# Every third low part of the weights in the second FFN loop, made by an accumulating transfer instead of VectorE

## What is computed

```python
h2 = _rms(x, g_norm2) * (1 + sc2) + sh2
gate, up = jnp.split(h2 @ w_ffn_in, 2, axis=-1)     # w_ffn_in: 2048 x 11264
x = x + gt2 * ((jax.nn.silu(gate) * up) @ w_ffn_out)  # w_ffn_out: 5632 x 2048
```

## Time and profile before

| | us |
|---|---|
| median of 2 runs | 2519.33 (2518.88 to 2519.78) |
| span of the profiled execution | 2517.7 |
| PE busy | 2440.5 (97%) |
| DVE busy | 1793.1 (71%) |
| ACT busy | 1082.6 (43%) |
| POOL busy | 223.2 (9%) |

### The profile page before, as it was taken

One profiled execution on the slowest core, in us unless ns is written; L12 is line 12 of the kernel. 1 busy time (PEld: TensorE's weight loads), 2 busy tenths in 40 slices (PEclk: granted clock), 3 DMA queues, 4 the chain that ended last, 5 costly groups with the idle time before them and its releaser, 6 DMA issues.

```text
span 2517.7 us, 30560 instructions
## 1 busy us (share of the span) xinstructions
PE 2440.5 (97%) x11620; PEld 2000.9 (79%) x11620; DVE 1793.1 (71%) x1751; ACT 1082.6 (43%) x1243; POOL 223.2 (9%) x397
## 2 busy tenths in 40 slices
PE   4899999999999999999999999999999999999999
PEld 3679448888888888879997778788788888888887
DVE  6878887888888888778785445865688555555565
ACT  2035124444444444464346557644544444444443
POOL 4412210111111111001110000000011000000000
PEclk8899999999999999999999999999999999999999
DMA  9999996898889888647985555355588555555654
GB/s 367 382 337 354 403 358 225 308 328 313 312 321 328 317 318 323 209 152 279 341 291 162 166 172 161 117 184 200 198 320 285 191 192 185 197 184 192 208 184 150
DMA packets 291262, 643.01 MB, mean 255 GB/s; under 512 B 21883, under 2 KB 34749, under 8 KB 290269
## 3 DMA queue, kind: packets, MB, share of 16 engines
q1 hardware_dynamic: 234512, 436.45, 50.8%
q0 software_dynamic: 56096, 205.02, 21.8%
q10 hardware_dynamic: 556, 0.18, 0.0%
HBM read 639.47 MB, written 2.13 MB: 255 GB/s over the span
## 4 chain that ended last, share of the span: by engine, by line
PE 86%; DVE 5%; DMA 4%; ACT 4%; issue 1%; POOL 0%; DVEq 0%; ACTq 0%; POOLq 0%
PE PS L1783 84%; DMA R<-in_w_ada 3%; DVE R L1093 2%; ACT WHI L580 1%; DVE WLO L1073 1%; DMA RAW<-in_w_ffn_gate 1%; PE PS L2013 1%; PE PS L1907 1%; PE PS L1938 0%; DVE H L1243 0%; ACT R L658 0%; ACT L945 0%; ACT L588 0%; DVE H L1242 0%; ACT L937 0%
## 5 line engine op out<-in xcount | busy, mean ns | idle before, releaser
L1073 DVE TENSOR_TENSOR WLO<-RAW,WHI 128x1024 fp32r<-128x1024 f32 x760 | 929.7, 1225 | 610.3 <-ACT WHI L580 608.0
L580 ACT ACTIVATE WHI<-RAW 128x1024 fp32r<-128x1024 f32 x760 | 805.5, 1061 | 1118.3 <-PE PS L1783 1103.0
L1783 PE MATMUL PS<-WHI,H 128*128 128x512 f32 x4064 | 1263.1, 392 | 5.7 <-DVE WLO L1073 5.0
L1783 PEld LDWEIGHTS PS<-WHI,H 128*128 128x128 f32 x4064 | 755.0, 188 | 173.8 <-DVE WLO L1073 16.0
L1783 PE MATMUL PS<-WLO,H 128*128 128x512 f32 x2032 | 792.1, 390 | 0.0
L1783 PEld LDWEIGHTS PS<-WLO,H 128*128 128x128 f32 x2032 | 381.4, 188 | 80.8
L1093 DVE SCALAR_TENSOR_TENSOR R<-R,CA 128x1024 f32<-128x1024 f32 x326 | 417.6, 1281 | 36.7 <-DMA R<-in_w_ada 29.7
L1783 PE MATMUL PS<-WHI,HID 128*128 128x512 f32 x1280 | 395.2, 390 | 0.0
L514 POOL DMA_DIRECT2D R<-in_w_ada x284 | 150.9, 531 | 1586.7 <-DVE R L1090 555.1
L1783 PEld LDWEIGHTS PS<-WHI,HID 128*128 128x128 f32 x1280 | 239.3, 188 | 49.0
L1783 PE MATMUL PS<-WLO,HID 128*128 128x512 f32 x640 | 249.1, 389 | 0.0
(11 more groups left out here) (233 smaller groups left out, 1233.7 us busy)
## 6 DMA issues: line engine op xcount, KB each, us to landing
R<-in_w_ada POOLq DMA_DIRECT2D x348, 512.0 KB, 6.7
RAW<-in_w_in SPq DMA_DIRECT2D x88, 1024.0 KB, 5.6
RAW<-in_w_ffn_in SPq DMA_DIRECT2D x88, 1024.0 KB, 5.0
RAW<-in_w_ffn_gate SPq DMA_DIRECT2D x44, 1024.0 KB, 6.9
RAW<-in_w_ffn_up SPq DMA_DIRECT2D x44, 1024.0 KB, 5.3
RAW<-in_w_ffn_down SPq DMA_DIRECT2D x44, 1024.0 KB, 8.3
RAW<-in_w_ffn_out SPq DMA_DIRECT2D x44, 1024.0 KB, 5.0
RAW<-in_w_out SPq DMA_DIRECT2D x32, 1024.0 KB, 7.3
```

The lines of the kernel that those rows point to most:

```text
L580: nc.scalar.activation(WHI[j][:, :, :], RAW[slot][:, 2 * half:2 * half + 2, :], ACT.Copy)\
L1073: nc.vector.tensor_tensor(WLO[j][:, :, :], RAW[slot][:, 2 * half:2 * half + 2, :], WHI[j][:, :, :].bitcast(F32), ALU.subtract).then_inc(lo ...
L1783: return nc.tensor.matmul(o, a, b, start=start, stop=stop, skip_group_check=True)
```

## The change

In turns 3 to 8 of the second layer's FFN, for the subs whose number counted from 616 leaves 2 when divided by 3 (48 of 144, 8 in a turn), DVE makes no low part. ACT writes WHI[j] as before and then, with a second pass over the same source, -RAW rounded to fp32r into WLO[j]. POOL waits for that (`neg_done`) and issues a transfer from RAW (SBUF) to WLO[j] (SBUF) that adds: WLO = -WHI + RAW. It counts `lo_pool` by 16 when it has landed, and PE waits for that semaphore ahead of such a sub. SP waits for both kinds of low part before it reloads a slot. PE counts the two kinds apart (`lows`, `pool_lows`). SP's loop is written out for layer two, since its waits differ from turn to turn, and ACT's loop starts at 3 instead of 2, with turn 2 written out, in both layers.

```diff
--- before.py
+++ after.py
@@ -116,6 +116,19 @@
+POOL_LO = (2 * U_FFN2 + 64, 2 * U_FFN2 + 64 + 24 * (NF - 5))
+def on_pool(s):
+    return POOL_LO[0] <= s < POOL_LO[1] and (s - POOL_LO[0]) % 3 == 2
+def pool_before(s):
+    return (max(0, min(s, POOL_LO[1]) - POOL_LO[0])) // 3
 def ring(s):
@@ -161,8 +174,10 @@
         self.quad, self.chain = Count(), Count()
+        self.lows, self.pool_lows = Count(), Count()
         self.all = dict(unit=self.unit, sub=self.sub, A=self.A, B=self.B, C=self.C, ada=self.ada,
-                        ada_group=self.ada_group, gate=self.gate, hid=self.hid, quad=self.quad, chain=self.chain)
+                        ada_group=self.ada_group, gate=self.gate, hid=self.hid, quad=self.quad, chain=self.chain,
+                        lows=self.lows, pool_lows=self.pool_lows)
@@ -290,6 +305,7 @@
         hi_done, lo_done, pe_sub = sem("hi_done"), sem("lo_done"), sem("pe_sub")
+        lo_pool, neg_done = sem("lo_pool"), sem("neg_done")
         pe_tb = sem("pe_tb")
@@ -353,7 +369,10 @@
                 elif last >= 0:
-                    sp.wait_ge(lo_done, c.unit.value(-3, times=2) - native_before(last))
+                    pooled_lows = pool_before(last + 2)
+                    sp.wait_ge(lo_done, c.unit.value(-3, times=2) - native_before(last) - pooled_lows)
+                    if pooled_lows:
+                        sp.wait_ge(lo_pool, 16 * pooled_lows)
                 c.unit.at += 1
@@ -389,11 +408,16 @@
                 down(0)
-                with sp.Fori(2, NF - 2) as i:
-                    c.enter(i - 2, unit=12)
-                    gate_up(i)
-                    down(i - 1)
-                c.leave(NF - 4)
+                if k == 3:
+                    for i in range(2, NF - 2):
+                        gate_up(i)
+                        down(i - 1)
+                else:
+                    with sp.Fori(2, NF - 2) as i:
+                        c.enter(i - 2, unit=12)
+                        gate_up(i)
+                        down(i - 1)
+                    c.leave(NF - 4)
                 gate_up(NF - 2)
@@ -558,6 +582,21 @@
+            def lows(n):
+                for s in range(n):
+                    if on_pool(c.sub.at):
+                        half, slot = c.sub.at % 2, c.sub.at // 2 % 4
+                        j, _ = ring(c.sub.at)
+                        pool.wait_ge(neg_done, c.pool_lows.value(1))
+                        pool.dma_start(WLO[j][:, :, :].bitcast(F32), RAW[slot][:, 2 * half:2 * half + 2, :], accum_op=ALU.add)\
+                            .then_inc(lo_pool, 16)
+                        c.pool_lows.at += 1
+                    c.sub.at += 1
+            c.sub.at = 2 * U_FFN2 + 64
+            lows(24 * (NF - 5))
@@ -579,6 +618,9 @@
                         .then_inc(hi_done, 1)
+                    if on_pool(c.sub.at):
+                        nc.scalar.activation(WLO[j][:, :, :], RAW[slot][:, 2 * half:2 * half + 2, :], ACT.Copy, scale=-1.0)\
+                            .then_inc(neg_done, 1)
                     c.sub.at += 1
@@ -742,10 +784,11 @@
                 body()
-                with act.Fori(2, NF - 2) as i:
-                    c.enter(i - 2, unit=12, sub=24, hid=1, gate=1)
+                body()
+                with act.Fori(3, NF - 2) as i:
+                    c.enter(i - 3, unit=12, sub=24, hid=1, gate=1)
                     body()
-                c.leave(NF - 4)
+                c.leave(NF - 5)
                 body(rows=True)
@@ -1069,9 +1112,10 @@
                     j, _ = ring(c.sub.at)
-                    dve.wait_ge(hi_done, c.sub.value(1) - native_before(c.sub.at))
-                    nc.vector.tensor_tensor(WLO[j][:, :, :], RAW[slot][:, 2 * half:2 * half + 2, :],
-                                            WHI[j][:, :, :].bitcast(F32), ALU.subtract).then_inc(lo_done, 1)
+                    if not on_pool(c.sub.at):
+                        dve.wait_ge(hi_done, c.sub.value(1) - native_before(c.sub.at))
+                        nc.vector.tensor_tensor(WLO[j][:, :, :], RAW[slot][:, 2 * half:2 * half + 2, :],
+                                                WHI[j][:, :, :].bitcast(F32), ALU.subtract).then_inc(lo_done, 1)
                     c.sub.at += 1
@@ -1782,10 +1826,20 @@
+            def low_ready(more=0):
+                at = c.sub.at + more
+                if on_pool(at):
+                    pe.wait_ge(lo_pool, c.pool_lows.value(1, times=16))
+                    c.pool_lows.at += 1
+                else:
+                    pe.wait_ge(lo_done, c.lows.value(1))
+                    c.lows.at += 1
             def sub(pair, src, k0, first, last, kind="W", counted=True):
                 (j, _), used, o = ring(c.sub.at), c.all[pair], PAIR[pair]
-                pe.wait_ge(lo_done, c.sub.value(1) - native_before(c.sub.at))
+                low_ready()
                 if first and used.at:
@@ -1825,7 +1879,7 @@
                                 middle()
-                            pe.wait_ge(lo_done, c.sub.value(i + 1) - native_before(c.sub.at))
+                            low_ready(i)
                         if i == 1:
@@ -2041,7 +2095,9 @@
                 with pe.Fori(3, NF - 2) as i:
-                    c.enter(i - 3, sub=24, A=2, C=2, hid=1, gate=1, ada_group=1 * beside)
+                    pooled_lows = 8 if k == 3 else 0
+                    c.enter(i - 3, sub=24, A=2, C=2, hid=1, gate=1, ada_group=1 * beside, lows=24 - pooled_lows,
+                            pool_lows=pooled_lows)
                     gate(previous)
```

## The result

| | before | after |
|---|---|---|
| median, us | 2519.33 (2518.88 to 2519.78) | 2628.01 (2627.02 to 2628.99) |
| span of the profiled execution, us | 2517.7 | 2627.3 |
| ratio, 95% interval | | 1.0431 (1.0414 to 1.0449) |

The account below looks back on a forecast made before the run. PE was taken to bound the loop, so relieving DVE gains nothing. 48 stalls of 5.8 - 2.92 = 2.88 us add 138 us to the 2517.7 us span, 2656, plus 1.6 for the median: 2658 us, range 2565 to 2860.

Parts of the forecast that it names:

- Bound and place: In the second layer's FFN loop PE never idles, so 59 us less DVE work saves nothing; turn about 89 us.
- Cover of 2.92 us: Time left for a pooled sub's transfer: 5.24 from copy start to use, less 2.02 and 0.30; any longer landing stalls PE.
- ACT's two passes and POOL's hand-over: Before each transfer: negated part ready 2.02 us after the copy's start, then 0.30 us until POOL issues.
- The two odd subs: Sixth sub of a turn gains 0.87 us of transposes, twelfth has Silu (1.03 us) ahead of its copy; about cancelling.
- L = 3.8 + 1.2 + 0.8: Accumulating transfer's time from POOL's issue to landing, 5.8 us, giving a stall of 2.88 us per pooled sub.
- The base: First part of the landing time: 3.8 us, the minimum of POOL's 512 KB loads before the loop.
- The second read: Accumulating transfer also reads its destination: 1.2 us, the 1 MB weight load's 5.0 less the 512 KB minimum 3.8.
- The collisions: Only the accumulate after the first of each six subs meets a moving weight load: about 0.8 us on average.
- Clock: Rival: TensorE's clock falls in the stalls, pooled subs running at 1.2 GHz: 131 us more, 2789 us; chance 0.12.
- The edits costed at nothing: SP's loop unrolled for layer two and one more turn of ACT's loop written out: no cost.
- That the transfer is hidden: Rival: landing under 3.96 us, as short as writes out of SBUF; less than 2% lost, 2520 to 2569 us; chance 0.11.
- That the add moves much more slowly than a copy: Rival: descriptors or adder set the rate; 2859 us at a 10 us landing, 3152 at 16.1; chance 0.20.

Follow-up runs that it names:

- experiment 10: Changed kernel with the addition left out, so POOL's 48 transfers only copy RAW over WLO: 2553.76 us, ratio 1.0142.
- experiment 9: Changed kernel with ten transposes of the identity into unused PSUM ahead of PE's wait for each transfer: 2616.21 us, ratio 1.0389.
- 1: Changed kernel with no sub marked for the transfer, DVE making every low part, loops still rewritten: 2519.82 us, ratio 0.9999.
- 2: Changed kernel with negated copies and transfers put into scratch tiles that nothing reads, DVE making all 144 low parts: 2520.06 us, ratio 1.0004.
- experiment 8: Changed kernel with half of each weight load left out in turns 3 to 8, nothing else: 2613.02 us, ratio 1.0372.
- experiment 3: Changed kernel with ACT making the negated copy before the high part, landings counted on four semaphores in turn: 2617.93 us, ratio 1.039.
- 4: Changed kernel with four WHI/WLO buffers instead of three in the six turns, landings counted on four semaphores: 2585.14 us, ratio 1.0254.
- 7: Changed kernel with the negated copy first, three buffers, and half of each weight load left out in turns 3 to 8: 2569.72 us, ratio 1.0196.
- 5: Changed kernel with four WHI/WLO buffers and half of each weight load left out in turns 3 to 8: 2543.75 us, ratio 1.0104.

## Why the prediction was right, and where its terms were off

**Bound and place.** Right. PE had no slack in the loop and DVE's relief was worth nothing; a new row of PE waits, released by the transfer, 48 times, is what the profile shows. Its mean is 1.69 us where 2.9 was forecast, a turn 84.3 us where 89 was. POOL was busy for 48 x 0.84 us, not 48 x 0.5: issuing an adding transfer takes it longer than the loads of the earlier trace rows.

**Cover of 2.92 us.** Nearly right: it is 2.77. One round in the changed kernel, from its chain of waits and (the middle line) PE's timeline:

```profile
1979.34 3.03 PE PS L1827 x12
...
1982.19 0.62 PE L1827 MATMUL PS<-WHI,H 128*128 128x512 f32 x2
...
1984.69 5.10 DMA WLO<-RAW
...
1989.83 4.62 PE PS L1827 x12
```

From the start of a pooled sub to the next issue it is 1984.69 - 1979.34 = 5.35 us, and from the landing (1989.79) to PE 0.04. Three subs at full pace are 8.16, which leaves 8.16 - 5.35 - 0.04 = 2.77. ACT's two passes and POOL's hand-over are as forecast (2.01 and 0.28). Two small terms were at nothing: a sub that starts after a stall takes 2.85 us and not 2.72 (the next one begins at 1982.19; the first two matmuls take 0.73 where two take 0.62), and the hand-over to PE. They make 48 x 0.15 = 7 us.

The mean of the 48 landings is 4.72 us, so the delay is 4.72 - 2.77 = 1.95 us per sub and 48 x 1.95 = 94 us in all. PE's idle rows show only 1.69, because the last matmul before a stall ends about 0.16 us after the next could have begun, and because of the slow start. The two odd subs stand out as worked out. In the second turn PE is idle for 0.58 us ahead of the sixth sub and 2.33 ahead of the twelfth, together about what two ordinary ones are. Their rows in its timeline:

```profile
2065.42 0.73 PE L1827 MATMUL PS<-WHI,H 128*128 128x512 f32 x2 [0.58 <-DMA WLO<-RAW]
...
2088.50 0.74 PE L1827 MATMUL PS<-WHI,H 128*128 128x512 f32 x2 [2.33 <-DMA WLO<-RAW]
```

**L = 3.8 + 1.2 + 0.8.** This is the term that was mis-sized. The base was too long: an undisturbed 512 KB copy inside SBUF by POOL lands in 2.8 to 2.9 us (experiment 10), less than any 512 KB load from memory in the earlier trace rows. The second read was somewhat too short: 1.2 forecast, about 1.6 measured between undisturbed landings, the longer issue on POOL included. The collisions were 0.8 forecast and came to 4.72 - 4.5 = 0.2. That every second transfer meets a load was right: in the chain of waits they take 4.5 us and more than that in turn. In sum 5.8 against 4.72, which makes 52 us too much. By the two rules of the Trainium skill (DMA: Bandwidth & Descriptors, the anatomy of one DMA on the gpsimd path; Collectives: The Full Stack, part 3) the estimates had been 3.2 us for the copy, which is the median of experiment 10 but lies between its two groups, and 4.4 for the adding one against 4.5 undisturbed. They were nearer than my row, which was of loads from memory and not from SBUF.

**Clock.** The sum left it out and a rival priced it at 131 us. It did happen, but at a few stalls only: 13.4 us by the stretches, 11.8 or somewhat more by experiment 9.

**What balances.** 94 for the transfer and 13 for the clock make 107 of 109 us. The same sum holds for two kernels that it was not made from: 48 x (4.51 - 2.77) + 8.5 = 92 us in experiment 8, where 93.3 were measured, and with 0.96 us more cover 48 x (5.31 - 3.73) + 22.0 = 98 us in experiment 3, where 98.9 were.

**How near the number came.** In part by luck. The landing was 52 us too much, the cover 7 too little and the clock 13 too little; the last two hid 20 of the 52, and what is left is, to within 2 us, the 30 between 2658 and 2628.

**The edits costed at nothing.** Right, by experiments 1 and 2.

**The rivals.** That the transfer is hidden: no, and even the copy was not, though with 34 us its time lies within that rival's 2520 to 2569. That the add moves much more slowly than a copy: it takes about twice the engine time, but at this size that lands it 1.4 to 1.6 us later and not at the 10 to 16.1 us of the rival. What the prediction did not see is that L depends on the stall. It took the landing as a number of the transfer. In fact a stall slows the weight loads and so keeps the DMA engines clear for the next transfer, and every us of stall taken away is partly given back as a longer landing: experiments 3 and 4 show it, and that it goes away with half of the loads in 7 and 5. Whether the loads come late because SP waits for the landing itself (`lo_pool`) or only because all engines run at PE's slower pace was not separated.

## What to carry to other kernels

Work moved off an engine that holds nobody up wins nothing, and if a transfer takes its place the transfer's whole latency goes on the ring: before such a move, take the time from a buffer's release to its use, subtract every hand-over (the one to the waiting engine and its slow start too), and compare with the landing of a transfer of the same kind, source and target. When the gap is closed by earlier issue or more buffers, measure the landing again beside the stream at full pace: the number read from a stalling kernel is a best case. And a deeper ring only helps instructions that nothing waiting stands ahead of in their engine's order.

## What the runs showed of the hardware that I had not expected

- A 512 KB copy from SBUF to SBUF issued by POOL lands in 2.8 to 4.4 us, median 3.2, in a kernel that still stalls for it; the 512 KB loads of POOL from memory beside the weights took 3.8 to 7.6.
- An accumulating transfer of the same size lands in 4.5 us undisturbed and keeps the 16 engines busy for 2.72 us against 1.30. Beside the stream at full pace it lands in 4.6 to 10.3 us, median 7.3.
- The granted clock did not follow the length of a single idle stretch alone. Of the 48 stretches in the changed kernel 14 were longer than 2.0 us. After eight of them (2.04 to 3.11 us) the sub took 4.4 to 4.6 us instead of 3.0, with a granted clock down to 0.50, the 1.2 GHz level, for about 3 us; after the other six (2.08 to 3.35 us, the longest of all among them) it did not, nor after any shorter one. In the chain of waits the sub after 2.04 us idle, at 1989.83, takes 4.62 us, the one after 2.35 us, at 2172.78, 3.03 us. Ten small matmuls in each stall kept it at 1.00 (experiment 9).
